# The last two expert blocks of a mixture-of-experts layer: their norm in slot order, the other tokens' on three engines

## The reference

```python
for e in range(N_EXPERTS):                       # 16 experts in 4 groups
    h = jax.nn.silu(xt @ w_gate[e]) * (xt @ w_up[e])
    out = out + gates[:, e:e + 1] * (h @ w_down[e])
...
moe = grouped_moe(x, w_router, b_router, w_exp_gate[l], w_exp_up[l], w_exp_down[l])
x = layer_norm(DN_ALPHA * x + moe, ln2_g[l], ln2_b[l])
```

## Time and profile before

| | |
|---|---|
| time of the runs | median 832.08 us (831.81 to 832.43) |
| the profiled execution | 832.42 us, its span 830.8 us |
| PE / DVE / ACT / POOL busy in the span | 818.4 / 579.1 / 450.8 / 72.2 us |
| transfers | 173.45 MB, mean 209 GB/s |

### The profile page before, as it was taken

How to read it: one execution, slowest core, us unless ns; L and a number is a source line. 1 busy time by engine, 2 the same in 40 slices (tenths; PEclk the granted TensorE clock), 3 DMA queues, 4 the chain that set the end, 5 groups by cost and what they waited for, 6 DMA issues and landing times.

```text
span 830.8 us, 11124 instructions
## 1 busy us (share of the span) xinstructions
PE 818.4 (99%) x3817; PEld 679.3 (82%) x3817; DVE 579.1 (70%) x675; ACT 450.8 (54%) x459; POOL 72.2 (9%) x73
## 2 busy tenths in 40 slices
PE   9999999999999999999999999999999999999995
PEld 8788888888888888888888888888888888888873
DVE  5877444434457885432456588898899899899978
ACT  4655524434466663333233333578877887878640
POOL 1000000100000000000000000622101111100121
PEclk9999999999999999999999999999999999999998
DMA  7332334553233333324522926799999999999582
GB/s 222 89 107 83 101 94 145 193 177 101 79 98 101 101 95 108 92 87 138 157 84 78 356 98 254 205 340 418 375 390 389 397 398 392 397 391 383 216 320 104
DMA packets 112354, 173.45 MB, mean 209 GB/s; under 512 B 7418, under 2 KB 90019, under 8 KB 100550
## 3 DMA queue, kind: packets, MB, share of 16 engines
q1 hardware_dynamic: 106502, 159.80, 54.5%
q0 software_dynamic: 5824, 13.30, 4.4%
HBM read 163.49 MB, written 16.30 MB: 216 GB/s over the span
## 4 chain that ended last, share of the span: by engine, by line
PE 95%; DVE 3%; DMA 1%; issue 0%; ACT 0%; DVEq 0%; SPq 0%
PE psA L713 8%; PE psA L712 8%; PE psA L711 8%; PE psA L898 7%; PE psA L900 7%; PE psA L899 7%; PE psB L713 6%; PE psB L711 6%; PE psB L712 6%; PE psB L925 3%; PE psB L923 3%; PE psB L924 3%; PE psD L713 2%; PE psD L711 2%; PE psC L713 2%; PE psC L711 2%
## 5 line engine op out<-in xcount | busy, mean ns | idle before, releaser
L1619 DVE TENSOR_TENSOR elo<-est,ehi 128x2048 fp32r<-128x2048 f32 x94 | 211.3, 2287 | 26.9 <-ACT ehi L1232 26.6
L1232 ACT ACTIVATE ehi<-est 128x2048 fp32r<-128x2048 f32 x94 | 177.7, 1917 | 42.9 <-DMA est<-in_w_exp_down_dram 27.9
L1404 DVE TENSOR_TENSOR wlo<-wst,whi 128x1024 fp32r<-128x1024 f32 (+1 forms) x75 | 93.8, 1251 | 85.0 <-ACT whi L1059 84.2
L1059 ACT ACTIVATE whi<-wst 128x1024 fp32r<-128x1024 f32 (+1 forms) x75 | 80.9, 1078 | 77.6 <-PE psB L713 30.7
L898 PE MATMUL psA<-ehi,xe_hi 128*128 128x512 f32 x256 | 101.4, 396 | 0.0
L900 PE MATMUL psA<-ehi,xe_lo 128*128 128x512 f32 x256 | 99.9, 390 | 0.0
L899 PE MATMUL psA<-elo,xe_hi 128*128 128x512 f32 x256 | 99.7, 389 | 0.0
L711 PE MATMUL psB<-xT_hi,whi 128*128 128x512 f32 x208 | 81.0, 390 | 0.0
L713 PE MATMUL psB<-xT_hi,wlo 128*128 128x512 f32 x208 | 80.9, 389 | 0.0
L712 PE MATMUL psB<-xT_lo,whi 128*128 128x512 f32 x208 | 80.9, 389 | 0.0
L900 PEld LDWEIGHTS psA<-ehi,xe_lo 128*128 128x128 f32 x256 | 48.1, 188 | 10.3
(11 more groups left out here) (375 smaller groups left out, 1532.5 us busy)
## 6 DMA issues: line engine op xcount, KB each, us to landing
est<-in_w_exp_gate_dram SPq DMA_DIRECT2D x32, 1024.0 KB, 12.2
est<-in_w_exp_up_dram SPq DMA_DIRECT2D x32, 1024.0 KB, 11.1
est<-in_w_exp_down_dram SPq DMA_DIRECT2D x32, 1024.0 KB, 12.6
wst<-in_w_in_dram SPq DMA_DIRECT2D x59, 512.0 KB, 3.9
wst<-in_w_branch_r_dram SPq DMA_DIRECT2D x8, 640.0 KB, 4.3
ys<-zero POOLq DMA_DIRECT2D x8, 512.0 KB, 2.9
wst<-in_w_branch_a_dram SPq DMA_DIRECT2D x8, 512.0 KB, 3.5
o_st<-in_w_out_dram SPq DMA_DIRECT2D x8, 512.0 KB, 4.4
```

The source lines that it names most:

```text
L1059: A(whi[p][:, 0:K, :], wst[p][:, 0:K, :], ACT.Copy).then_inc(w_hi, 1)
L1232: A(ehi[s][:], est[s][:], ACT.Copy).then_inc(gu_hi if s < 4 else d_hi, 1)
L1404: V.tensor_tensor(wlo[p][:, 0:K, :], wst[p][:, 0:K, :], whi[p][:, 0:K, :], ALU.subtract).then_inc(w_lo, 1)
L1619: V.tensor_tensor(elo[s][:], est[s][:], ehi[s][:], ALU.subtract).then_inc(gu_lo if s < 4 else d_lo, 1)
```

## The change

It does five things.

1. **Order.** Block b takes expert `ORDER[b]`: the first three experts of each group in blocks 0 to 11, then the fourth of each group. Blocks 14 and 15 hold experts 11 and 15, of groups 2 and 3, so that no token is in both.
2. **Late rows.** The tokens of blocks 14 and 15 are handled as they lie in the block's slots: POOL gathers their other expert's row from `ys` into `late[p]` (index list `other`), adds the gathered `xe[p]` to it, DVE adds the block's scaled result (`late_half`), and the norm is done on `late[p]`. An indirect transfer writes them to the output, after all four token tiles have been stored.
3. **The other tokens.** POOL loads each tile's first-expert rows (`first_y`) during the last two turns and adds them to `x1` (`add_first`), later the later-expert rows `later_y` of tiles 0 to 2 (DVE those of tile 3). ACT computes mean and squares of the rows with its accumulator (`mean_and_square`) and normalises tiles 0 and 2 and `late[0]` (`norm_row`); POOL multiplies and adds `ln2` for these (`gain`); DVE does it for tiles 1 and 3 and `late[1]` (`finish`).
4. **No 0/1 sums.** The matrices and PE's 44 matmuls of `by_prev`, `own` and `by_last` are gone, and so are the splits of the two results.
5. **Weights of the last down.** They go to buffers of their own (`dl_raw`), loaded as soon as DVE has made the low part of block 15's first gate pieces, and are rounded and split ahead of `hidden(15)`. In turn 14 ACT does `y_out(13)` and `hidden_round` ahead of `e_round(14, 4)` and `(14, 5)`.

```diff
+    LATE = NE - 2
+    ORDER = [g * GRP + e for g in range(NG) for e in range(GRP - 1)] + [g * GRP + GRP - 1 for g in range(NG)]
...
+            e = expert if expert is not None else ORDER[b] if of is None else of
...
+            for n in range(2):
+                sp.wait_ge(gu_lo, 4 * (NE - 1) + 1 + n)
+                sp.dma_start(dl_raw[n][:], w_exp_down[0, ORDER[NE - 1]].rearrange("(p k) n -> p k n", p=P)
+                             [:, 2 * n:2 * n + 2, :].rearrange("p k (a n) -> p (k a) n", n=DF)
+                             ).then_inc(last_landed[n], 16)
...
+            for t in range(TT):
+                sp.dma_start(later_y[t][:], ys[t * P:(t + 1) * P, :]).then_inc(got[t], 16)
+            sp.wait_ge(d_lo, 2 * LATE + 1)
             load_ln2(ln2_landed)
...
+            sp.wait_ge(out_pool, 1)
+            store_row(0)
+            sp.wait_ge(out_dve, 1)
+            store_row(1)
+            sp.wait_ge(out_dve, 2)
+            store_row(3)
+            sp.wait_ge(out_pool, 2)
+            store_row(2)
...
+            def add_first(t):
+                nc.gpsimd.tensor_tensor(x1[:, t, :], x1[:, t, :], first_y[t % 2][:], ALU.add).then_inc(first_added, 1)
...
+                if b == NE - 1:
+                    pool.wait_ge(y_stored[0], 6 * 16)
+                    pool.wait_ge(y_stored[1], 5 * 16)
+                    load_first(0)
+                    load_first(1)
+                    for p in range(2):
+                        pool.wait_ge(row_landed[p], 16)
+                scatter(b - 4, lists[:, b - 4, 1:2].bitcast(U32))
+            for p in range(2):
+                add_first(p)
+            pool.wait_ge(first_added, 2)
+            pool.wait_ge(y_stored[1], 6 * 16)
+            load_first(2)
+            load_first(3)
...
+                pool.wait_ge(row_landed[p], 32)
+            scatter(12, lists[:, 12, 1:2].bitcast(U32))
+            for t in (2, 3):
+                add_first(t)
+            pool.wait_ge(first_added, TT)
+            pool.wait_ge(other_done, 1)
+            pool.wait_ge(y_stored[0], 7 * 16)
+            for p in range(2):
+                pool.indirect_dma_start(out=late[p][:], out_offset=None, in_=ys[0:ROWS, :],
+                                        in_offset=bass.IndirectOffsetOnAxis(ap=other[:, p:p + 1], axis=0),
+                                        bounds_check=ROWS - 1, oob_is_err=False).then_inc(row_landed[p], 16)
+            for p in range(2):
+                pool.wait_ge(row_landed[p], 48)
+            scatter(13, lists[:, 13, 1:2].bitcast(U32))
+            for p in range(2):
+                pool.wait_ge(xe_t, NE - 1 + p)
+                nc.gpsimd.tensor_tensor(late[p][:], late[p][:], xe[p][:], ALU.add).then_inc(late_row, 1)
+            for t in range(TT - 1):
+                pool.wait_ge(got[t], 16)
...
+            def gain(row, n, done):
+                pool.wait_ge(fin_norm, n + 1)
+                nc.gpsimd.tensor_tensor(row, row, ln2_gb[:, 0, :], ALU.mult).then_inc(fin_gain, 1)
+                pool.wait_ge(fin_gain, n + 1)
+                nc.gpsimd.tensor_tensor(row, row, ln2_gb[:, 1, :], ALU.add).then_inc(done, 1)
+            gain(x1[:, 0, :], 0, out_pool)
+            gain(x1[:, 2, :], 1, out_pool)
+            gain(late[0][:], 2, out_pool)
+            pool.wait_ge(stored, 16 * TT)
+            for p, done, count in ((0, out_pool, 3), (1, out_dve, 3)):
+                pool.wait_ge(done, count)
+                pool.indirect_dma_start(out=out2, out_offset=bass.IndirectOffsetOnAxis(
+                                            ap=lists[:, LATE + p, 1:2].bitcast(U32), axis=0),
+                                        in_=late[p][:], in_offset=None, bounds_check=S - 1,
+                                        oob_is_err=False).then_inc(late_stored, 16)
+            pool.wait_ge(late_stored, 32)
...
+            b = NE - 2
+            e_round(b + 1, 0)
+            e_round(b + 1, 1)
+            silu(b)
+            rows_round(b + 1)
+            e_round(b + 1, 2)
+            e_round(b + 1, 3)
+            for s in range(2):
+                y_out(b - 1, s)
+            hidden_round(b)
+            e_round(b, 4)
+            e_round(b, 5)
...
+            def last_round(n):
+                act.wait_ge(last_landed[n], 16)
+                act.wait_ge(gu_used, 4 * (NE - 1) + 2)
+                A(dl_hi[n][:], dl_raw[n][:], ACT.Copy).then_inc(d_hi, 1)
+            def mean_and_square(row, u, n):
+                if n:
+                    act.wait_ge(fin_sq, n)
+                A(unread[:], row, ACT.Identity, scale=-1.0 / D, accum_out=fin[:, 1, u:u + 1]).then_inc(fin_mean, 1)
+                act.wait_ge(fin_mean, n + 1)
...
+            last_round(0)
+            last_round(1)
+            act.wait_ge(gu_used, 4 * (NE - 1) + 3)
+            act.wait_ge(row_sum, 1)
+            mean_and_square(x1[:, 0, :], 0, 0)
+            act.wait_ge(row_sum, 2)
+            mean_and_square(x1[:, 1, :], 1, 1)
             act.wait_ge(h_t, NE)
-            act.wait_ge(y_stored[0], (NE // 2 - 1) * 16)
...
             A(h15_hi[:], psC[1][:, 0, :].rearrange("p (k c) -> p k c", c=P), ACT.Copy).then_inc(h_h, 1)
...
+            root(0, 0)
+            root(1, 1)
+            act.wait_ge(row_sum, 3)
+            mean_and_square(x1[:, 2, :], 2, 2)
+            norm_row(x1[:, 0, :], 0, 1)
+            act.wait_ge(row_sum3, 1)
+            mean_and_square(x1[:, 3, :], 3, 3)
+            root(2, 2)
+            root(3, 3)
+            norm_row(x1[:, 2, :], 2, 3)
+            act.wait_ge(late_sum, 2)
+            mean_and_square(late[0][:], 4, 4)
+            root(4, 4)
+            norm_row(late[0][:], 4, 5)
+            root(5, 5)
...
+            for p in range(2):
+                ins = V.tensor_copy(other_f[:, p:p + 1], lists[:, LATE + p, 1:2])
+            chain.link(ins)
+            V.tensor_scalar(other[:], other_f[:], float(S), None, ALU.add).then_inc(other_done, 1)
...
+            def rstd_of(u, count):
...
+                dve.wait_ge(std_done, TT + count)
+                chain.link(V.reciprocal(fin[:, 5, u:u + 1], fin[:, 4, u:u + 1]))
+                chain.link(V.tensor_scalar(fin[:, 5, u:u + 1], fin[:, 5, u:u + 1], fin[:, 3, u:u + 1],
+                                           fin[:, 4, u:u + 1], ALU.mult, ALU.add))
+                chain.link(V.reciprocal(fin[:, 6, u:u + 1], fin[:, 5, u:u + 1]))
+                V.tensor_tensor(fin[:, 7, u:u + 1], fin[:, 1, u:u + 1], fin[:, 6, u:u + 1], ALU.mult
+                                ).then_inc(fin_rstd, 1)
+            def finish(row, u, cols=slice(0, D)):
+                chain.link(V.scalar_tensor_tensor(row[:, cols], row[:, cols], fin[:, 1, u:u + 1], ln2_gb[:, 0, cols],
+                                                  ALU.add, ALU.mult))
+                return V.scalar_tensor_tensor(row[:, cols], row[:, cols], fin[:, 6, u:u + 1], ln2_gb[:, 1, cols],
+                                              ALU.mult, ALU.add)
...
+            def late_half(p, ps, s):
+                half = late[p][:, s * DF:(s + 1) * DF]
+                V.scalar_tensor_tensor(half, ps[s], lists[:, LATE + p, 2:3].bitcast(F32), half,
+                                       ALU.mult, ALU.add).then_inc(late_sum, 1)
...
             last_weights(0)
+            last_weights(1)
             hidden(NE - 1)
+            dve.wait_ge(got[TT - 1], 16)
+            dve.wait_ge(first_added, TT)
+            V.tensor_tensor(x1[:, TT - 1, :], x1[:, TT - 1, :], later_y[TT - 1][:], ALU.add).then_inc(row_sum3, 1)
             dve.wait_ge(h_h, NE)
...
                             ALU.subtract).then_inc(h_l, 1)
-            last_weights(1)
...
+            for u in range(2):
+                spread_of(u, fin[:, 2, u:u + 1], u + 1)
+            for u in range(2):
+                rstd_of(u, u + 1)
+            dve.wait_ge(ln2_landed, 32)
+            dve.wait_ge(fin_rstd, 2)
+            finish(x1[:, 1, :], 1).then_inc(out_dve, 1)
+            dve.wait_ge(d_used, 2 * LATE + 2)
+            dve.wait_ge(late_row, 1)
...
+                late_half(0, psB, s)
+            for u in (2, 3):
+                spread_of(u, fin[:, 2, u:u + 1], u + 1)
+            for u in (2, 3):
+                rstd_of(u, u + 1)
+            dve.wait_ge(fin_rstd, 4)
+            finish(x1[:, 3, :], 3).then_inc(out_dve, 1)
+            spread_of(4, fin[:, 2, 4:5], 5)
+            rstd_of(4, 5)
+            dve.wait_ge(late_row, 2)
...
+                if s == 0:
+                    dve.wait_ge(half_down, 1)
+                else:
+                    dve.wait_ge(d_used, NE * 2)
+                late_half(1, psA, s)
+                dve.wait_ge(late_sum, 3 + s)
+                ins = V.bn_stats(fin_bn[:, 0, 6 * s:6 * s + 6], late[1][:, s * DF:(s + 1) * DF])
+            chain.link(ins)
+            bn_moments(5).then_inc(var_done, 1)
+            rstd_of(5, 6)
+            dve.wait_ge(fin_rstd, 6)
+            finish(late[1][:], 5).then_inc(out_dve, 1)
```

323 lines of the change are left out of this document (131 added, 192 removed).

## The result

The changed kernel took 856.07 us (median of four executions, 852.62 to 857.68), the kernel before on the same chip 832.21: a ratio of 1.0282, 95% interval 1.0249 to 1.0315. Slower was forecast, and by late row sums that hold `h_hi` back; but the forecast was 843, and 856 lies outside its range. The study has to find 13 us. One thing is already different in the spread: the four executions of the kernel before lie within 1 us, those of the changed one within 5.

The account below looks back on a forecast made before the run. It took PE as the bound, then 26.7 us of DVE norms and store. 11.7 us of delay ahead of `h_hi`, 7.2 of waits, 20.3 of DVE and 4.6 of store replaced these: 843 us, range 829 to 849.

Parts of the forecast that it names:

- Part 1: Expert order, dropped 0/1 sums, small added pieces: worth nothing; the small pieces 1 us if not covered by PE's work.
- The mechanism: At the last down: `h_hi` 11.7 us later behind two row sums on ACT, PE standing 7 us, DVE's chain ending last.
- Part 2: POOL's chain to the scatter of block 13: issued at 791.3, landed at 795.9, 0.8 us later than before; `later_y` from 799.5.
- I take 9.7 for the direct ones: Landing time in us assumed for POOL's direct first-row loads while transfers are full, from the `lists<-tab` row.
- Part 3: POOL adds and two-SBUF-input DVE instructions exclude each other; free in the turns, but after the gathers `hb` comes at 798.0, not 794.45.
- Instruction by instruction, in the order of asking: The rule for POOL and DVE sharing SBUF: each excludes the other for one instruction, first asker first; 4.4 us of the sum.
- Part 5: DVE's new end from 809.1: norms with 7.2 us of waits for POOL to 836.6, then the indirect store to 841.2.
- the same 0.4 us to the end: After the last store lands at 841.2, the span was to end 0.4 us later, as before, at 841.7.
- in short: Summary: 11.7 us delay ahead of `h_hi`, 7.2 of waits, a new end of 20.3 DVE plus 4.6 store, instead of 26.7.
- not exclusive: Rival: POOL and DVE don't exclude each other; `h_hi` at 806.0, no 7.2 us of waits, 834.5 us; chance 0.13.
- the rows come early: Rival: late gathers and scatter land sooner, `h_hi` at 800.3; without exclusion 828 us, faster; chance 0.15.
- Slower than forecast: Rival: scatter and last store take 8.6 us as in the turns, `h_hi` 3.3 later, 850 us; chance 0.10.

## Why the prediction was right and wrong

- **Part 1, order and small pieces free:** right for the order (1.0003); the small pieces were not run by themselves.
- **The mechanism, `h_hi` behind two row sums, PE waiting for `h_lo`, DVE's chain as the end:** seen in the trace as written. PE's wait was hidden, as the forecast said, even at twice the length.
- **Part 2, the step that failed: the time that POOL needs to reach scatter 13 and the row adds.** Two terms were too small. The first is "I take 9.7 for the direct ones", which was used for both loads of a pair. The first of each pair took 10.2 and 7.8 us, the second 13.4 and 11.0. From the first load's issue to the scatter behind the pair were 14.8 and 12.4 us where the forecast had 10.3 and 10.4; with 1.6 us of smaller delays scatter 12 stood at 780.92, not 772.8. The second is a term put at nothing: in the turns only DVE was made to wait, not POOL. From scatter 12 to the first late gather the forecast had 8.7 us, for the landing alone; there were 15.1, since the issue took 9.52 and the two adds 4.77. That is 14.5 us of delay. The gathers gave back 1.2 (both had landed at 804.66, 6.0 us after the issue of the second at 798.62, where 8.6 were taken), and what lies between scatter 13 and the row adds 2.0: scatter 13 at 804.66 instead of 791.3, the row adds at 811.79 instead of 800.4. These 11.4 us are those by which `h_hi` is later than the forecast.
- **Part 2 followed one path where two ended together.** In its own sum the rows landed at 799.5 and POOL's adds ended at 800.4. In the changed kernel POOL's adds ended at 810.33 and the row adds began at 811.79. So scatter 13 out at 783.00 made them start 2 us earlier, no more: POOL's own list of adds and gathers held them.
- **Part 3, exclusion:** right in kind, in both directions. "Instruction by instruction, in the order of asking" was wrong. POOL's two adds went back to back from 790.46 to 795.23 while DVE's split of 791.27 waited (8.32 us for two of 2.2). The Trainium skill, SBUF — State Buffer, "Who interferes with whom", says that whoever issues first has the ports for the whole instruction; the trace agrees, but here the holder also kept them for its next instruction. The same section of the Trainium skill infers that a two-input instruction of VectorE leaves descriptor generation alone. Here the traces differ and decide: an issue of POOL's beside one ended 0.9 us after it, and took 2.97 us instead of 1.0.
- **Part 5, DVE's end:** 25.75 us against 27.5 forecast, with 6.9 us of waits against 7.2. This was the best term. Taking POOL's passes away gave back 6.5.
- **The last store:** 3.3 us to land instead of 4.6, but "the same 0.4 us to the end" was 5.9. That is 5.5 us, and no row of before could show it.
- **The sum.** The DVE chain ended 9.5 us after its forecast (11.3 from the late rows, 1.8 back from a shorter chain), the store 9.0, the span 14.4. (The profiled execution is 1.6 us above the median, so of the time it is 13.) The sentence "in short" sets the new end, counted from `h_lo`, against 26.7 us counted from PE's last expert matmul; from the end of `h_lo` (797.30) the old end is 33.5 us. The 843 didn't use this comparison.
- **The rivals.** Neither "not exclusive" nor "the rows come early" happened. "Slower than forecast", put down to slow transfers, was the near one, but with a chance of 0.10 and 850 it held one of three causes.

Open: why the issue of scatter 12 is kept out for one, two or four splits in the changed kernel and never for more than one in 33 held scatters of the kernel before. That the spread of the time hangs on when the adds behind it run is supported by the kernel with held adds, which lost the spread, and by the profiles above. That the second load of each pair took 11 to 13 us because it shares the transfers with the weights (busy all the time in both stretches, 743 to 758 and 768 to 781 us) was not tried.

## What to carry over

Before giving an engine that issues in order more work, write down its whole list with durations up to the instruction that somebody waits for: here moving a transfer 22 us forward won nothing, because the instruction that others wait for stood behind 23 us of other work, and of waiting for its own gathers, on the same engine (786.28 to 809.55). Work of VectorE and GpSimd that reads two SBUF operands should be summed, not overlapped, in the tail too, down to products of one number. And don't let an indirect store of GpSimd's be the last transfer of a program: it cost 4 to 5 us in both kernels.
